# TensorE transposes of a gated DeltaNet layer replaced by a DMA exchange and VectorE block transposes

## The reference, cut to what matters

```python
h = rms_norm(x, norm1_g); proj = h @ w_in
qkv_c = silu(causal_depthwise_conv(qkv, conv_w))      # 4 taps along the tokens, one filter per channel
q, k = l2_normalize(q), l2_normalize(k)
o = gated_delta_rule(q, k, v, g, beta)                # chunks of 64 tokens, a triangular solve in each
o = rms_norm(o, norm_g) * silu(z)
y_gdn = o @ w_branch_gdn
```

## Time and profile before

| | |
|---|---|
| median of 3 runs | 1782.39 us (1782.3 to 1782.4) |
| the profiled execution | 1781.72 us |
| its span | 1779.8 us |
| TensorE busy in the span | 1762.3 us (99%) |
| VectorE busy | 1264.3 us (71%) |
| ScalarE busy | 853.1 us (48%) |
| granted TensorE clock, mean | 0.999 |
| DMA moved | 316.49 MB, 178 GB/s in the mean |

### The profile page before, as it was taken

How to read it: one execution, slowest core, us unless ns; L and a number is a source line. 1 busy time by engine, 2 the same in 40 slices (tenths; PEclk the granted TensorE clock), 3 DMA queues, 4 the chain that set the end, 5 groups by cost and what they waited for, 6 DMA issues and landing times.

```text
span 1779.8 us, 27113 instructions
## 1 busy us (share of the span) xinstructions
PE 1762.3 (99%) x9974; PEld 1432.9 (81%) x9974; DVE 1264.3 (71%) x1903; ACT 853.1 (48%) x1345; POOL 96.3 (5%) x81
## 2 busy tenths in 40 slices
PE   8999999999999999999999999999999999999998
PEld 6887787777777888888888888888888888888886
DVE  5578688787886677775676697888644468886444
ACT  6454454554645455554444454454443345444443
POOL 0021030030210000000000000000000000000000
PEclk9999999999999999999999999999999999999999
DMA  7544444444444545445666565555666555556554
GB/s 265 176 156 133 155 151 138 160 143 143 137 136 161 178 153 168 155 154 187 204 210 201 198 217 186 192 189 195 205 191 197 192 192 194 192 189 198 192 191 140
DMA packets 88118, 316.49 MB, mean 178 GB/s; under 512 B 9728, under 2 KB 10496, under 8 KB 87888
## 3 DMA queue, kind: packets, MB, share of 16 engines
q1 hardware_dynamic: 86608, 311.20, 52.6%
q0 software_dynamic: 832, 3.15, 0.5%
q10 hardware_dynamic: 576, 0.71, 0.1%
HBM read 312.92 MB, written 2.10 MB: 177 GB/s over the span
## 4 chain that ended last, share of the span: by engine, by line
PE 93%; DVE 6%; issue 1%; ACT 0%; DMA 0%; POOLq 0%; POOL 0%; ACTq 0%; DVEq 0%
PE acc L347 29%; PE acc L348 28%; PE acc L349 28%; DVE cT L1207 2%; DVE w_lo L1176 1%; PE J L526 1%; PE J L578 1%; PE J L411 1%; PE J L404 1%; PE J L435 1%; PE J L540 1%; PE J L455 0%; PE J L550 0%; PE J L597 0%; PE J L445 0%
## 5 line engine op out<-in xcount | busy, mean ns | idle before, releaser
L1176 DVE TENSOR_TENSOR w_lo<-raw,w_hi 128x1024 fp32r<-128x1024 f32 x584 | 712.5, 1227 | 352.5 <-ACT w_hi L776 349.7
L776 ACT ACTIVATE w_hi<-raw 128x1024 fp32r<-128x1024 f32 x584 | 617.0, 1062 | 648.2 <-PE acc L349 641.3
L347 PE MATMUL acc<-w_hi,hT_hi 128*128 128x512 f32 x1440 | 577.3, 401 | 2.3 <-DVE w_lo L1176 1.5
L348 PE MATMUL acc<-w_lo,hT_hi 128*128 128x512 f32 x1440 | 562.7, 391 | 0.0
L349 PE MATMUL acc<-w_hi,hT_lo 128*128 128x512 f32 x1440 | 561.9, 390 | 0.0
L347 PEld LDWEIGHTS acc<-w_hi,hT_hi 128*128 128x128 f32 x1440 | 270.7, 188 | 67.4 <-issue 7.0
L349 PEld LDWEIGHTS acc<-w_hi,hT_lo 128*128 128x128 f32 x1440 | 270.9, 188 | 57.8
L348 PEld LDWEIGHTS acc<-w_lo,hT_hi 128*128 128x128 f32 x1440 | 271.1, 188 | 52.7 <-issue 1.0
L347 PE MATMUL acc<-w_hi,act_hi 128*128 128x512 f32 x512 | 199.2, 389 | 0.0
L348 PE MATMUL acc<-w_lo,act_hi 128*128 128x512 f32 x512 | 199.2, 389 | 0.0
L349 PE MATMUL acc<-w_hi,act_lo 128*128 128x512 f32 x512 | 199.2, 389 | 0.0
(11 more groups left out here) (234 smaller groups left out, 1341.1 us busy)
## 6 DMA issues: line engine op xcount, KB each, us to landing
raw<-weights SPq DMA_DIRECT2D x584, 512.0 KB, 3.4
xres<-x POOLq DMA_DIRECT2D x4, 512.0 KB, 4.8
xres<-x SPq DMA_DIRECT2D x3, 512.0 KB, 8.9
y<-nat SPq DMA_DIRECT2D x6, 256.0 KB, 3.7
fgain_sb<-fgain SPq DMA_DIRECT2D x1, 1024.0 KB, 5.5
masks_sb<-masks POOLq DMA_DIRECT2D x1, 704.0 KB, 8.1
xres<-x SPq DMA_DIRECT2D x2, 256.0 KB, 5.3
y<-nat ACTq DMA_DIRECT2D x2, 256.0 KB, 3.1
```

Of the source, the lines that this page charges most:

```text
L347: mm(o, aT_hi[:, kt, tok], w_hi[:, c % RING, w], start=first, stop=False)
L348: mm(o, aT_hi[:, kt, tok], w_lo[:, c % RING, w], start=False, stop=False)
L776: A(w_hi[:, slot], raw[:, slot], ACT.Copy).then_inc(hi_ready, 1)
L1176: tt(w_lo[:, slot], raw[:, slot], w_hi[:, slot].bitcast(F32), ALU.subtract).then_inc(lo_ready, 1)
```

## The change

Five of the seven kinds of DeltaNet turns leave TensorE: the raw K, Q and V (`PE_FRONT`), the turn back of Q for its squares, and the turn of the outputs (`PE_OT`). K's and V's turn back stay. In their place:

- **Fronts.** ScalarE and VectorE write `rawg` in an order by quarters of 32 columns. SyncE's queue writes the 512 KB to a scratch tensor in HBM (`front_write`) and reads them back with the quarters of the partitions exchanged (`front_read`, eight DMAs of 64 KB with runs of 512 B). One VectorE transpose of 32x32 blocks over 128x1024 (`take_front`) puts the turned item into `rawg`, from where `conv` and `tap` read it (from SBUF now, not from PSUM). They stand at h = 37, 46 and 61 of the item's own window.
- **Squares of Q and outputs.** The block transpose comes first (`DVE_BACK_Q` at h = 19, `DVE_OT` at 58), then one write and four reads (`quarters`). `q_squares` on ScalarE moves from 22 to 36 and its use on VectorE (`DVE_NQ`) from 23 to 40. `og_hi` and `og_lo` of a group move from h = 62 and 63 to h = 13 of the next window (72 for the last group), and VectorE writes `og_lo` in eight instructions of 128 columns where four of 256 were.
- **SyncE.** The loop over chunks in this stage becomes a written-out list with the exchange's DMAs and waits between the weight loads.

```diff
-PE_FRONT = {ITEM_K: -8, ITEM_Q: 17, ITEM_V: 54}
-PE_BACK = {ITEM_K: 17, ITEM_Q: 49, ITEM_V: 80}
-PE_ROWS, PE_KK, PE_KQ, PE_QT, PE_OT = 11, 29, 46, 82, 124
+PE_BACK = {ITEM_K: 17, ITEM_V: 80}
+PE_ROWS, PE_KK, PE_KQ, PE_QT = 11, 29, 46, 82
-ACT_NSQ = {ITEM_K: 8, ITEM_Q: 22}
+ACT_NSQ = {ITEM_K: 8, ITEM_Q: 36}
+DVE_FRONT = {ITEM_K: 37, ITEM_Q: 46, ITEM_V: 61}
+SP_OUT, SP_BACK = (17, 25, 33), (19, 27, 35)
+SP_Q, SP_O, SP_DIST = (20, 22), (38, 40), 4
-DVE_ROWS, DVE_NK, DVE_KK, DVE_EYE, DVE_KQM, DVE_NQ, DVE_VB, DVE_Z = 4, 7, 14, 17, 18, 23, 35, 41
+DVE_ROWS, DVE_NK, DVE_KK, DVE_EYE, DVE_KQM, DVE_NQ, DVE_VB, DVE_Z = 4, 7, 14, 17, 18, 40, 35, 41
-DVE_OSUM, DVE_OSCALE, DVE_OT = 56, 56, 63
+DVE_OSUM, DVE_OSCALE, DVE_BACK_Q, DVE_OT = 56, 56, 19, 58
+OG_AT = (77, 77, 77, 72)
...
+            def front_write(k):
+                w, n = divmod(k, 3)
+                sp.wait_ge(rawg_a, 4 * w + n + 1)
+                sp.wait_ge(rawg_d, 4 * w + n + 1)
+                if k > 1:
+                    sp.wait_ge(front_T, k - 1)
+                sp.dma_start(bounce[k % 2], rawg[:, n].rearrange("p t n -> p (t n)")).then_inc(front_out, 16)
+            def front_read(k):
+                sp.wait_ge(front_out, 16 * (k + 1))
+                if k:
+                    sp.wait_ge(front_T, k)
+                if k > 2 and k % 3 == ITEM_Q:
+                    sp.wait_ge(nsq_done, 2 * (k // 3))
+                kept = bounce[k % 2].rearrange("(q j) (t p f) -> j p t q f", j=Q, t=NT, p=P // Q)
+                for p in range(P // Q):
+                    for t in range(NT):
+                        sp.dma_start(fronts[k % 3 % 2][p * Q:(p + 1) * Q].rearrange("j (t q f) -> j t q f", t=NT, q=P // Q)[:, t],
+                                     kept[:, p, t]).then_inc(front_in, 16)
+            def quarters(dst, kept, done):
+                for to in range(P // Q):
+                    sp.dma_start(dst[to * Q:(to + 1) * Q].rearrange("i (r f) -> i r f", r=P // Q),
+                                 kept.rearrange("(r i) (p f) -> i p r f", i=Q, p=P // Q)[:, to]).then_inc(done, 16)
+            def turn_back(c, g):
+                if c == SP_Q[0]:
+                    sp.wait_ge(q_T32, g + 1)
+                    sp.dma_start(q_bounce, rawg[:, ITEM_Q].rearrange("p t n -> p (t n)")).then_inc(q_out, 16)
+                if c == SP_Q[1]:
+                    sp.wait_ge(q_out, 16 * (g + 1))
+                    quarters(q_rows, q_bounce, q_in)
...
+                    sp.wait_ge(lo_ready, c - RING + 1)
+                    sp.dma_start(raw[:, c % RING], weights[c]).then_inc(raw_in[c % RING], 16)
...
+            def take_front(n, g):
+                k = 3 * g + n
+                dve.wait_ge(front_in, 16 * 8 * (k + 1))
+                V.transpose(front(n).rearrange("p m (b j) -> p b m j", j=Q),
+                            fronts[n % 2].rearrange("p (b m i) -> p b m i", m=HG, i=Q)).then_inc(front_T, 1)
...
+                if h == DVE_BACK_Q:
+                    dve.wait_ge(silu_done, 4 * g + 2)
+                    V.transpose(rawg[:, ITEM_Q].rearrange("p t n -> p (t n)").rearrange("p (r u i) -> p r u i", r=P // Q, u=U),
+                                qU.rearrange("p (u r j) -> p r u j", r=P // Q, u=U)).then_inc(q_T32, 1)
                 if h == DVE_OT:
-                    dve.wait_ge(o_T, g + 1)
+                    dve.wait_ge(on_done, g + 1)
+                    V.transpose(vb[:].rearrange("p t n -> p (t n)").rearrange("p (q u j) -> p q u j", q=P // Q, u=U),
+                                vU.rearrange("p (u q i) -> p q u i", q=P // Q, u=U)).then_inc(o_T32, 1)
+            def og_step(h, g):
+                if g >= 0 and h == OG_AT[g]:
...
+                            for a in range(2):
+                                ins = stt(out=lo[:, :, a], in0=o_turned(g, b, par)[:, :, a], scalar=gdn_gain,
+                                          in1=hi[:, :, a].bitcast(F32), op0=ALU.mult, op1=ALU.subtract)
```

148 lines of the change are left out of this document (85 added, 63 removed).

## The result

| | before | after |
|---|---|---|
| median of the runs | 1782.35 us (1781.26 to 1782.40, 4 runs) | 1800.28 us (1798.28 to 1800.58, 4 runs) |
| ratio | | 1.0101, 95% interval 1.0089 to 1.0113 |
| the profiled execution | 1781.72 us | 1798.28 us |
| span | 1779.8 us | 1796.5 us |
| mean granted clock of TensorE | 0.999 | 0.994 |

The changed kernel is 1.0% slower, where 0.2% faster was forecast, and lies above the forecast's range: 21.5 us over the forecast by the medians. The profiled execution is the fastest of its four; the other three took 1800.27 to 1800.58 us, at a granted clock of 0.993.

A forecast was written before the change was run, and what follows sets the result against it. VectorE, arriving just as TensorE wants it, was taken to bound the kernel. Gains 0.9 + 1.5 - 0.3 + 0.6 + 0.9 = 3.6 us took 1781.72 to 1778.1; plus 0.67 for the median, 1778.8 us, range 1764.5 to 1786.5.

The forecast's parts named there:

- the fourth margin: At chunk 19, w_lo ends at 293.70 and the product starts at 293.76: no margin for a later VectorE.
- What TensorE gives up: 160 transposes in 20 turns leave TensorE at 0.88 us a turn: 17.6 us, the upper end of the gain.
- What VectorE gets: Block transposes at 1.34 us each, og_lo 2.2 us for 1.6, taps cheaper: 5.2 us more VectorE work per window.
- Rival B: Block transposes on VectorE are dear; at twice the length 8.8 us slower, 1791.2 us; chance 0.15.
- what is saved: a tap reads SBUF, 418 for 476 ns: VectorE's taps get shorter by reading SBUF: 0.058 us each, 0.7 us for the twelve of an item.
- (1): First edge, window 0 to 1: K's front turn goes and VectorE has few jobs there; gain 0.9 us.
- (4): Inside group 0: chunk 11 keeps its 0.88 us, level 1 is late by 0.4; gain 0.6 us.
- (2): Three later edges: VectorE's row before SiLU of K 0.5 us shorter, TensorE waits 1.2; gain 0.5 each, 1.5 us.
- (3): Inside groups 1 to 3: waits at chunk 11 and inversion level 1 swallow the gains; loss 0.1 each, 0.3 us.
- What costs nothing: Squares at h = 36, transposes in the recurrence and SyncE's 37 more DMAs a window stay covered: zero cost.
- Rival C: The exchange's reads land late, 65 us each, fronts overrun by some 45: 2320 us in all; chance 0.03.
- Rival D: The change doesn't do what it says, TensorE's sequence held elsewhere: within 1 us of 1782.4; chance 0.04.

The follow-up runs named there:

- short_turns: Kernel before, with most transposes of the front turns, Q's turn for its squares and the outputs' turn cut, nothing put in their place: 1774.44 us, ratio 0.9958.
- moved_into_gaps: Changed kernel with og_hi/og_lo of groups 0 to 2 at step 82, Q's block transpose for squares at 28, V's rows at 70: 1788.05 us, ratio 1.0035.
- v_rows_at_70: Changed kernel with only V's block transpose moved, to step 70 in place of 61: 1795.51 us, ratio 1.0080.
- filled_waits: Changed kernel with sixteen unused transposes on TensorE ahead of K's turn back and of chunk 11's products, groups 1 to 3: 1798.00 us, ratio 1.0092.
- q_taps_sbuf: Kernel before, with one operand of Q's taps read from SBUF (rawg) in place of PSUM (J): 1787.45 us, ratio 1.0032.
- masks_after_taps: moved_into_gaps, with GpSimd waiting for Q's second tap before its last two mask products and the power behind them: 1787.54 us, ratio 1.0036.

## Why the prediction was wrong

*What bounds the kernel.* Right. The places where VectorE arrives just in time were the right ones, all three, and short_turns shows that two of them (K's turn back and the levels) held back 6.0 of 14.1 us even with nothing added. Chunk 19, the fourth margin, takes 2.86 us in both kernels.

*What TensorE gives up.* Right: 20 turns, 0.88 us each. With 17.6 us the account of the spans closes to 0.6 us (in moved_into_gaps, v_rows_at_70 and filled_waits it leaves 2.6 to 3.6 us open).

*What VectorE gets.* The block transposes were right as an instruction (1.24 us), in part by luck, since the sum scaled a row of 32 partitions by a price per column taken from other operations. They were too dear by 0.18 us, the 0.1 that I added for a missing overlap and the 0.08 of an overlap that is there: in window 3 one starts at 348.18 and the split behind it at 349.34, 1.16 us later. Rival B is out. `og_lo` was right. **The step that failed is "what is saved: a tap reads SBUF, 418 for 476 ns".** I took the gap between two groups for the price of PSUM, though they differ in more than that (a tap's scalar is a column, SiLU's is a constant). From SBUF a tap lasts 475 ns. The 0.7 us saved an item, 2.1 us a window, were not there. And the same sentence held the larger error: moving the operand to SBUF made both inputs SBUF, beside GpSimd. That made Q's first taps 1128 ns: 2.65 us a group, in a row where the forecast put GpSimd at nothing without a reason. K's second tap met a mask product too, 2.45 us for four instead of 1.65:

```profile
353.88 2.45 DVE L1272 SCALAR_TENSOR_TENSOR cT<-rawg,cwg,cT 128x254 f32<-128x254 f32 x4
```

The trace of before had the sign, and I had not read GpSimd at all, since it is busy 5%. Its mask products have one shape and two lengths:

```profile
L1764 POOL TENSOR_TENSOR mats<-scg,masks_sb 128x512 f32<-128x512 f32 x4 | 7.8, 1958 | 2.5 <-DVE scg L1271 2.5
...
L1766 POOL TENSOR_TENSOR mats<-mats,masks_sb 128x512 f32<-128x512 f32 x4 | 5.2, 1304 | 0.0
```

The long one starts at 243.97, 0.17 us into a `w_lo` split (243.80, 1.22 us), which has both its inputs in SBUF. That GpSimd waited there for the split is an inference from the two rows; that it does so with the taps is shown by q_taps_sbuf and masks_after_taps.

*Place by place.* (1) The first edge gave its 0.9 us (chunk 30 of window 0 takes 2.72 for 3.61). Another 0.8 us came at chunk 0, before any step of the change, and is no part of it: the kernel's first products start 0.43 us apart instead of 0.23 for a while, until 13.8 us before and until 12.0 after, though the clock column says 1.00 there. Over the profiled executions of all kernels chunk 0 takes 4.6 to 6.5 us, so no account of spans here is better than that. (4) Inside group 0 a gain of 0.6 was forecast, and 2.2 us were lost, most at chunks 10 to 12 of window 1 (3.92, 4.79 and 6.31 us for 2.72, 4.64 and 5.31). (2): TensorE waits before K's turn back three times, but 2.5 us, not 1.2. From the scaling (341.09) to SiLU of K (363.03) VectorE takes 21.9 us, where it took 21.4 and where I had 20.9: the 0.7 of the taps and the 0.8 of the collision, less 0.4 for two block transposes that were priced too high. (3): the wait before chunk 11 is 2.0 to 2.9 us, not 0.9, for the same reasons with 2.65 us of collision; the wait ahead of a level is 1.8 us, forecast at 2. In all 26.7 us of waiting for 14.3.

*A term that was missing.* The forecast priced a wait at its length. Behind five of the nine waits of 1.8 us and more in windows 2 to 4 the granted clock went to half, 1.7 us each, 8.5 us. By engine time the larger waits (11 us more than forecast, 25.2 - 14.3) and the clock (8.5) make 19.4 us; the miss, by the spans, is 16.7 + 3.6 = 20.3. By place, half of it lies in one stretch: from K's turn back to chunk 11 the forecast had no change in windows 2 to 4, and the three stretches grew by 2.9, 3.4 and 3.8 us, 10.1 in all, and with the whole clock there, in v_rows_at_70, they grow by 9.3 just the same: it is VectorE's row with Q's taps. So the taps beside GpSimd are the failed step, and the clock comes second, with some 3.8 us that reached the time.

The Trainium skill (TensorE: Matmul & The Clock Gate, HAM oscillation — how this bites in real kernels) warns that idle gaps of TensorE, if they are long enough, bring its clock down. The trace agrees in kind: 0.66 behind the waits, 1.00 elsewhere. But the page's rule is for longer gaps than these; here 2.0 to 2.5 us were enough in five places.

*What costs nothing.* Held. The squares at h = 36 and SyncE's 37 DMAs a window made no new wait of TensorE in the changed kernel (ScalarE's `w_hi` waits for weights 7.9 us in all, where it waited 3.6, at most 1.7 at a time), and a read of 64 KB landed after 2.4 to 2.6 us:

```profile
bounce<-rawg SPq DMA_DIRECT2D x12, 512.0 KB, 5.5
og_hi<-bounce SPq DMA_DIRECT2D x64, 64.0 KB, 2.6
og_lo<-bounce SPq DMA_DIRECT2D x32, 64.0 KB, 2.4
```

Rival C is out. But that cover was thinner than I had it: three steps later for Q's block transpose and ScalarE waits 52 us. Rival D is out too. (The DMA share in the earlier trace rows is 0.44, where the prediction reads 0.43; nothing rests on it.)

What stays open: why a tap with its scalar in a column lasts 475 ns and SiLU's instruction of the same width 418; which waits bring the clock down and which do not; and the 2.6 to 3.6 us that the account of the spans leaves in three of the other kernels.

## What to carry to other kernels

When an operand moves from PSUM to SBUF, list what GpSimd does at that moment, however little it is busy: an instruction of VectorE that then has both inputs in SBUF waits out GpSimd's. Price a new wait of TensorE at more than its length, since the clock may fall behind it, but count the fall (1.4 to 1.7 us here) only where TensorE sets the time of the next place; where VectorE sets it, the fall is waited away. Moves that relieve the same place are worth more together than one by one. Work that leaves TensorE for VectorE pays only where VectorE waits; here the same exchange was 1.0% slower or 0.3% faster by where it stood in VectorE's order and by one part of five.

## What was unexpected of the hardware

A tap with one operand in PSUM runs beside GpSimd's products at 475 ns, and with both in SBUF at 1128 ns in the mean (q_taps_sbuf 1129, the changed kernel 1128); a long one ends 0.3 us behind a product. GpSimd's products were longer too: 1476 for 1304 ns in q_taps_sbuf, with nothing changed but that operand. A block transpose of 128x1024 lasts 1.24 us, 2.8 times one of 32x256 (435 ns) for sixteen times the elements. And 10.6 us of work more on TensorE, put into its waits, made the kernel no slower (1798.00 against 1800.28 us).
